# A hybrid trunk step on one core: other weights in the weave of expert groups into the latent tokens' mixers

## The reference

```
h  = rmsnorm(x) * (1 + sc1) + sh1
u  = h @ w_in                              # 1024 -> 2584 columns, split among four mixers
y  = [ssd(u), gated_delta(u), fourier(u), windowed_attention(u)] @ w_out
x  = x + g1 * y
h2 = rmsnorm(x) * (1 + sc2) + sh2
q  = h2 @ w_q                              # 1024 -> 2048, 8 heads x 2 halves x 128
s  = q . sub_keys ; top 16 of 128 for each half ; top 16 of the 16 x 16 sums   -> idx, gate
act = gelu(sum_d peer_u[idx][d] * h2[d])   # 128 rows of peer_u per token
x  = x + g2 * sum_e gate*act * peer_v[idx] # 128 rows of peer_v per token
```

## Time and profile before

| | |
|---|---|
| median of 3 runs | 3334.72 us (3332.95 to 3336.97) |
| the profiled execution | 3323.2 us, its span 3321.4 us |
| DVE busy | 1769.2 us (53%) |
| PE busy | 1944.2 us (59%) |
| POOL busy | 1725.5 us (52%), nearly all gathers |
| DMA, queue of the gathers | 805.40 MB, 66.9% of 16 engines' span |
| unit 1 | 360 to 1044 us |
| unit 2 | 1044 to 1892 us |
| unit 3 | 1892 to 2566 us |
| tail | 2566 us to the end |

### The profile page before, as it was taken

The page is one execution under the profiler, slowest core; times in us unless marked ns, Lnnn a source line. Parts: engine busy times, 40 slices in busy tenths (PEclk is TensorE's granted clock), DMA queues, the critical chain, the costliest instruction groups (busy, mean ns, idle before and its releaser), DMA issues.

```text
span 3321.4 us, 27774 instructions
## 1 busy us (share of the span) xinstructions
PE 1944.2 (59%) x10194; PEld 1140.6 (34%) x10194; DVE 1769.2 (53%) x3951; ACT 360.2 (11%) x801; POOL 1725.5 (52%) x1540
## 2 busy tenths in 40 slices
PE   5888476657873321348878684676892000057787
PEld 4667365544642311331233163562660000001111
DVE  2423688862178988960013388873149888830000
ACT  2222111102111000000010011111210000000000
POOL 0000374434344777876545574444342877766665
PEclk9879687767996555679989996777896555579999
DMA  7557495546886998899999897546784999999998
GB/s 288 178 183 315 156 393 178 178 141 239 290 292 229 370 411 283 301 320 367 361 334 365 299 353 259 178 152 214 252 319 148 336 367 367 379 358 366 355 364 317
DMA packets 249064, 959.26 MB, mean 289 GB/s; under 512 B 32353, under 2 KB 33505, under 8 KB 231137
## 3 DMA queue, kind: packets, MB, share of 16 engines
q0 software_dynamic: 221184, 805.40, 66.9%
q1 hardware_dynamic: 19584, 142.62, 11.4%
q10 hardware_dynamic: 8160, 9.46, 0.8%
HBM read 955.01 MB, written 2.36 MB: 288 GB/s over the span
## 4 chain that ended last, share of the span: by engine, by line
POOL 25%; PE 25%; DVE 21%; DMA 13%; issue 13%; ACT 3%; ACTq 1%; another core or an unknown queue 0%; POOLq 0%; DVEq 0%
POOL sb_ring L486 25%; PE pb L509 16%; DMA sb_ring<-in_peer_v,sb_idxT 10%; PE pv L509 7%; DVE sb_ring L1803 6%; DMA sb_ring<-in_peer_u,sb_idxu 2%; PE pb L512 1%; DVE sb_pos L1715 1%; ACT sb_big L989 1%; DVE sb_big L1710 1%; ACT sb_hT L989 1%; DVE sb_big L1502 1%; DVE sb_big L1374 1%; DVE sb_big L1521 1%; DVE sb_big L1762 1%
## 5 line engine op out<-in xcount | busy, mean ns | idle before, releaser
L486 POOL DMA_INDIRECT sb_ring<-in_peer_u,sb_idxu x768 | 980.5, 1277 | 861.5 <-PE pv L509 399.1
L486 POOL DMA_INDIRECT sb_ring<-in_peer_v,sb_idxT x768 | 744.7, 970 | 714.9 <-PE pv L509 464.6
L1803 DVE CUSTOM_DVE_ANT_0 sb_ring<-sb_ring,sb_h 128x1024 f32<-128x1024 f32 x768 | 916.3, 1222 | 141.3 <-DMA sb_ring<-in_peer_u,sb_idxu 108.4
L509 PE MATMUL pv<-sb_ring,sb_wcol 128*32 128x512 f32 x3072 | 754.9, 646 | 174.4 <-DMA sb_ring<-in_peer_v,sb_idxT 139.6
L509 PE MATMUL pb<-sb_hT,sb_wring 128*128 128x256 f32 (+1 forms) x1920 | 383.7, 361 | 106.5 <-ACT sb_cinP L989 62.3
L509 PEld LDWEIGHTS pb<-sb_hT,sb_wring 128*128 128x128 f32 x1920 | 328.8, 207 | 180.8 <-issue 72.4
L509 PEld LDWEIGHTS pv<-sb_ring,sb_wcol 128*32 128x32 f32 x3072 | 134.5, 114 | 732.8 <-DMA sb_ring<-in_peer_v,sb_idxT 501.2
L509 PE MATMUL pb<-sb_big 128*128 128x128 f32 (+2 forms) x1888 | 257.4, 308 | 114.9 <-DVE sb_big L1502 80.6
L509 PEld LDWEIGHTS pb<-sb_big 128*128 128x128 f32 (+1 forms) x1888 | 250.4, 218 | 126.8 <-DVE sb_big L1502 85.6
L512 PE MATMUL pb<-sb_cst,sb_dots 128*128 128x128 f32 x6 | 2.7, 452 | 397.3 <-DVE sb_dots L1809 393.3
L1816 DVE COPY sb_accv<-pv 128x1024 f32<-128x1024 f32 x6 | 7.3, 1225 | 386.9 <-PE pv L509 373.7
(11 more groups left out here) (219 smaller groups left out, 1816.9 us busy)
## 6 DMA issues: line engine op xcount, KB each, us to landing
sb_wring<-in_w_in_blocks SPq DMA_DIRECT2D x32, 1024.0 KB
sb_ring<-in_w_mod_blocks SPq DMA_DIRECT2D x30, 1024.0 KB, 5.1
sb_wring<-in_w_q_blocks SPq DMA_DIRECT2D x27, 1024.0 KB
sb_wring<-in_w_mod_blocks SPq DMA_DIRECT2D x18, 1024.0 KB
sb_wring<-in_w_out_blocks SPq DMA_DIRECT2D x13, 1024.0 KB
sb_ring<-in_peer_u,sb_idxu POOLq DMA_INDIRECT x768
sb_ring<-in_peer_v,sb_idxT POOLq DMA_INDIRECT x768
sb_ring<-in_w_in_blocks SPq DMA_DIRECT2D x8, 1024.0 KB, 6.2
```

What stands on the lines that cost most here:

```text
L486: pool.indirect_dma_start(ring[:, j, :], None, a["tab_" + kind][l_of(q)], bass.IndirectOffsetOnAxis(ap=of, axis=0)).then_inc(rows_in[j], 16)
L509: return nc.tensor.matmul(out, lhsT, rhs, start=start, stop=stop)
L1803: dve.tensor_tensor_reduce(out=ring[:, j, :], in0=ring[:, j, :], in1=h2[:, t, :], scale=1.0, scalar=0.0, op0=ALU.mult, op1=ALU.add, accum_ ...
```

## The change

Only weights in `mix_points` change, for the units of the latents (g = 1, units 1 and 3). The weights are relative: the sum over the unit's points is scaled to its 64 groups. The scan's points 0 to 5 get the weight 0, and the last entry of the list (the stage's end that the extra call appends) is taken away again.

```
-    add("scal", [0, 1], 4, 4)
+    add("scal", [0, 1], 3 if g else 4, 3 if g else 4)
     add("pre", [0], 3, 5)
     for i in range(nt):
-        add(f"intra{i}", [0, 1, 2, 3, 4, 5, 6, 7, 8, 9], 5, 3)
-    add("scan", range(8) if g else [6, 7], 5, 5)
+        add(f"intra{i}", [0, 1, 2, 3, 4, 5, 6, 7, 8, 9], 3 if g else 5, 0 if g else 3)
+    if g:
+        add("scan", range(6), 0)
+        pts.pop()
+    add("scan", [6, 7], 5, 5)
     add("fnet", [], 1, 5)
     add("attp", [0], 4, 5)
     for i in range(nt):
         add(f"att{i}", range(3), 4, 3)
-    add("out", range(8), 2 * nt, 2)
-    add("query", range(17), 2 * nt, 4)
-    for i in range(nt):
-        add(f"topk{i}", range(10), 2, 4)
+    if g:
+        add("out", range(8), 0)
+        add("query", range(17), 1, 2)
+        for i in range(nt):
+            add(f"topk{i}", range(10), 4, 4)
+    else:
+        add("out", range(8), 2 * nt, 2)
+        add("query", range(17), 2 * nt, 4)
+        for i in range(nt):
+            add(f"topk{i}", range(10), 2, 4)
```

## The result

The changed kernel takes 3302.85 us (median of 4 runs, 3294.87 to 3309.6) where the kernel before takes 3335.84 on the same chip: a ratio of 0.9895, 95% interval 0.9865 to 0.9925. It is about 33 us faster. The forecast was 3312, so right in sign and 9 us too high.

The account below looks back on a forecast made before the run. Bounds differ by stage: DMA in the projection, PE in the query, DVE in top-k. Terms summed to -8.6 us (unit 1) and -14.6 (unit 3), together -23: 3312 us on the median's basis, range 3288 to 3340.

Parts of the forecast that it names:

- Projection, +27: Input projection: five more u groups at 5.4 us each, since DMA is full there; +27 us per unit.
- Rival A: Extra u groups cost only DVE time: projection grows by 20, attention's +3 isn't seen; 3292 us, chance 0.16.
- Rival B: Projection takes the pace of DMA shared with weight blocks: 42 instead of 27 per unit; 3342 us, chance 0.10.
- The 5.4 from units 2 and 3: Projection: price per u group, from 29 groups in unit 2 against 14 in unit 3, 81.0 us for fifteen.
- Scalar and intra, +4, -10 and 0: Per unit: scalar stage's group moved forward +4, fewer u groups in intra stages -10, gelu and first v group 0.
- Burst behind the scan, -25: Between scan and attp: three v groups beginning earlier cut DVE's wait from 35 to about 10 us; -25 per unit.
- rival D: Before attp: the burst's wait stays, DVE still standing 30 us, 20 less gain per unit; 3352 us, chance 0.05.
- Before the scores, -3.6: Ahead of attention's scores: the v group there goes, saving 3.6 us per unit.
- Softmaxes, +3: Attention: two v groups per softmax instead of one, the second of att1 waiting for rows; +3 us per unit.
- Output projection and query, -18: Output projection and query: four and seven fewer v groups, ten on PE's path at 1.8 us; -18 per unit.
- Top-k, +14 and +8: Top-k: ten more v groups, limited by gathers; +14 us in unit 1, +8 in unit 3.
- rival C: Top-k goes at POOL's pace, DVE products stretching gathers: 16 more per unit; 3344 us, half of it 3328; chance 0.11.

Follow-up runs that it names:

- the burst experiment: The changed kernel with five v groups in one burst behind the scan again, none at intra1's end, one fewer in the query: 3302.5 us, ratio 0.9945.
- the early part: Changed kernel's order up to attention (u groups, gelu, v groups), nearly the old order from the output projection on: 3300.2 us, ratio 0.9899 to the kernel before.
- the late part: Kernel before with only later v groups moved: none in output projection, 3 in query, 17 in top-k: 3325.3 us, ratio 0.9967.

## Why the prediction was right

The burst behind the scan, the largest gain, went by its mechanism, and so did the output projection and the query. That the total came within 9 us is owed to luck as well: the projection's price had the wrong reason, the softmaxes the wrong sign, and the errors offset each other in part.

*Projection, +27: measured +23.3.* A group costs 4.5 to 4.7. The forecast priced it as its transfer in a full DMA; the rows fit DVE's own work better. The whole stage of unit 1, before and after:

```profile
381.82:490.16 108.34, 81.28 (x352) 68.51 (x352) 91.87 (x163) 18.77 (x43) 75.89 (x55) 0.90 0.90 346
```

```profile
388.72:520.60 131.88, 84.04 (x352) 70.23 (x352) 115.86 (x203) 18.92 (x43) 97.95 (x75) 0.84 0.94 366
```

The stage is 23.5 us longer and DVE is busy 24.0 longer in it; the time in which it stands is 16.5 and 16.0. Where a group's rows are there in time, the group takes DVE 4.58 us, from its first operation to what follows it:

```profile
427.38 1.22 DVE L1812 CUSTOM_DVE_ANT_0 sb_ring<-sb_ring,sb_h 128x1024 f32<-128x1024 f32 x1
...
431.96 0.38 DVE L1380 TENSOR_SCALAR sb_big<-sb_cinS,sb_lay 128x256 f32<-128x256 f32 x1
```

Five are 22.9. DMA is nearly full beside it (in the windows above its share went from 0.97 to 1.00), but it still moved more per us, 366 GB/s against 346 over the stage. Five transfers of 5.79 would be 29, or 26 less the 3 us that DMA still had free at 0.97, and 23.3 were measured. No run separates DVE from DMA here, so that DVE sets the price is argued from these rows and not shown. Rival A, the u groups cost only DVE's time, gave 20 for the projection, as near as the forecast, and had attention's +3 not come, as it didn't; its time of 3292 is 11 too low where the forecast's is 9 too high. Rival B (42) is out. The 5.4 from units 2 and 3 was misread besides: the convolutions take DVE 25.1 us in unit 3 and 18.5 in unit 2, so fifteen groups cost 87.6 us between them, 5.8 each.

*Scalar and intra, +4, -10 and 0: +2.3 and -10.2.* Gelu with the first v group at intra1's end was taken at nothing, but the v group costs 3.7 there (the burst experiment). The emptier levels and ends, with gelu's new place, gave 13.9 and not 10. The two errors cancel.

*Burst behind the scan, -25: -22.7, and +1.0 for the v groups inside the scan.* The step held, and rival D is out. The prediction put PE's start 10 us ahead of the norms' end, it is 9.9, and the wait at about 10, it is 12.36. It did not name gelu's product on DVE as the cause of PE's late start; by the burst experiment about half of this step's gain goes with it.

*Before the scores, -3.6: -2.9. Softmaxes, +3: -2.3.* The second is the term with the wrong sign. The gathers are behind, as forecast: PE waits for rows in both softmaxes. But the forecast kept the matmuls' durations of before, at a mean granted clock of 0.72. At 0.99 all that follows the softmax is shorter, and this outweighs the waits.

*Output projection and query, -18: -16.6 and -22.0.* Blocks 3.45 us apart everywhere, and 2.1 per group in the output projection (8.2 for four). Unit 3 gained 5.4 more than unit 1: before's query took 109.1 us there and 103.7 in unit 1, and after the change the two are 95.2 and 95.4.

*Top-k, +14 and +8: +15.4 and +16.3.* In unit 1 the size was right, in unit 3 half of it. (The prediction's 93 us after the scores give +10.4 and +5.0 against before, not +10.7 and +5.4; it changes 14 to 13.) From 947.17 to 1026.58 POOL issues 52 gathers of unit 1, so 79.41 / 51 = 1.56 each, 6.23 us a group where the forecast had 5.79. For 13 groups that is 5.7 us, a third of rival C's 16. Its mechanism is there, and shown below.

*Sum.* Forecast -8.6 and -14.6, measured -13.9 and -16.2; of the 6.9 between them 10.7 is the softmaxes' sign and 7.4 the projection, against 9.7 in top-k. The diff as a whole did what it was forecast to do, but the experiments put the credit elsewhere: by the stages the early part has -29.8 and the late part nothing. The late part traded 21.0 us of PE's (output and query, without the early part) for 19.2 of the gathers' in top-k. The forecast had it at -4 and -10.

## What to carry to other kernels

Side work that one queue feeds has a price that depends on the stretch: here 4.5 us for a u group in a stage where both DVE and DMA are nearly full, 0.5 to 1 in one where DVE waits for PE; for a v group 1.6 for three and then 3 each in one where PE is full, and 3.7 in a stage whose own work has got shorter than the gathers. Spread it until these prices are equal; moving all of it from one full stretch to another trades one bound for the next. Reckon the price by each engine's own time as well as by the queue whose share is highest: here five groups cost their 23 us of DVE and not their 29 of transfers. And where a chain of small steps opens a burst, look at what it is queued behind: of the 22.7 us that the wait before attp lost, 10.8 went with moving one 128x128 product from behind the norms.

## What the runs showed of the hardware

A gather's issue takes 0.94 us, and stretches beside DVE operations that have two inputs in SBUF. In the trace of after 365 of the 1536 issues take over 1.05 us. POOL and DVE, unit 3, top-k:

```profile
2484.50 0.94 POOL L495 DMA_INDIRECT sb_ring<-in_peer_v,sb_idxT  x1 [0.30 <-issue]
2485.74 1.89 POOL L495 DMA_INDIRECT sb_ring<-in_peer_v,sb_idxT  x1 [0.30 <-issue]
2487.94 2.02 POOL L495 DMA_INDIRECT sb_ring<-in_peer_v,sb_idxT  x1 [0.30 <-issue]
2490.26 0.94 POOL L495 DMA_INDIRECT sb_ring<-in_peer_v,sb_idxT  x1 [0.30 <-issue]
...
2484.49 2.33 DVE L1771 TENSOR_TENSOR sb_big<-sb_big,sb_cst 128x2048 f32<-128x2048 f32 x1
2486.86 2.29 DVE L1775 TENSOR_TENSOR sb_big<-sb_big,sb_ke 128x2048 f32<-128x2048 f32 x1
2489.18 2.29 DVE L1777 TENSOR_REDUCE sb_big<-sb_big 128x128 f32<-128x2048 f32 x1
```

The first product ends at 2486.82 and the gather beside it at 2487.63, the second at 2489.15 and its gather at 2489.96: both 0.81 later. Beside the reduction, 0.94. The one at 2484.50, 0.01 us after a product's start, isn't held. The Trainium skill, SBUF — State Buffer, "Who interferes with whom", says that a DVE instruction with two SBUF inputs contends with a GpSimd instruction that reads SBUF, and calls the shared pair of ports an exclusive lock; the rows agree in that the held gathers end at a fixed distance from the product's end. The same section infers that such a product leaves the making of DMA descriptors alone; here it holds the issue of gathers, and the measurement decides. In top-k the price is mild: at most one gather per product waits, at most 1.95 us more, and ten such gathers in unit 1's top-k add 11 us to POOL's time while DMA still moves data at a share of 0.94.

Most of the stretched issues, 308 of the 365, stand beside the multiply-and-sum of a u group, which also reads two tensors in SBUF, and end 0.8 us after it. POOL in unit 1's projection, beside the group at 427.38:

```profile
427.55 1.86 POOL L495 DMA_INDIRECT sb_ring<-in_peer_u,sb_idxu  x1 [0.30 <-issue]
```

It ends at 429.41, the operation at 428.60. Over the whole program a gather of u takes POOL 1.25 us and one of v 0.99 (1.28 and 0.97 before), so the change didn't bring this about.

The clock was the other surprise. More work on PE in attention made attention shorter: at six groups instead of four the granted clock was 0.98 and 0.99, not 0.72 (of the levels 1.2 and 2.4 GHz), and it fell back to 0.68 and 0.71 when two groups were taken out again. The first products behind unit 3's first softmax, before and after:

```profile
2311.31 0.96 PE L509 MATMUL pb<-sb_qkv,sb_big 128*128 128x64 f32 x4
```

```profile
2298.05 0.56 PE L518 MATMUL pb<-sb_qkv,sb_big 128*128 128x64 f32 x4
```

The eight such rows of a tile take 5.2 us from first to last before (2311.31 to 2316.53) and 2.8 after (2298.05 to 2300.85), so 2.4 us less for each tile. In the two softmaxes PE also waits for rows, which takes part of it back.
